# Query and key projections of the gated-memory mixer computed token-major, turned back through DRAM, with the modulation sums shared out differently

## The reference, cut to what matters

```python
proj = x @ w_in                                    # x [256, 2048]
qk, v, o, gates, z = split(proj)                   # qk has 2048 columns: 1024 for q, 1024 for k
qk = silu(causal_depthwise_conv(qk, conv_w, conv_b))   # 4 taps along the tokens, one filter a column
q, k = split(qk)                                   # 8 heads of 128 each
cell = mlstm_chunkwise(q, k, v, gates...)          # needs q and k with their features on the rows
...
mod = silu(c) @ w_ada + b_ada                      # one row of 6 * 2048 numbers for the second block
```

## Time and profile before

| | us |
|---|---|
| median of 3 runs | 2192.4 (2192.33 to 2195.02) |
| the profiled execution | 2195.33 |
| its span | 2193.4 |

### The profile page before, as it was taken

The page is one execution under the profiler, slowest core; times in us unless marked ns, Lnnn a source line. Parts: engine busy times, 40 slices in busy tenths (PEclk is TensorE's granted clock), DMA queues, the critical chain, the costliest instruction groups (busy, mean ns, idle before and its releaser), DMA issues.

```text
span 2193.4 us, 32090 instructions
## 1 busy us (share of the span) xinstructions
PE 2170.4 (99%) x10814; PEld 1840.6 (84%) x10814; DVE 1514.1 (69%) x2046; ACT 1019.5 (46%) x1251; POOL 297.4 (14%) x555
## 2 busy tenths in 40 slices
PE   9999999999999999999999999999999999999998
PEld 8898888988778887899888888888888888888886
DVE  6766668877777877688776768776666666554544
ACT  5445544554444546434555544454444444444433
POOL 2101110112220010701110211111111111000000
PEclk9999999999999999999999999999999999999999
DMA  8877577688996584968766887767878887765564
GB/s 291 240 193 245 174 260 245 198 227 287 299 297 190 176 303 143 263 204 263 229 187 193 285 277 239 237 222 237 268 253 278 268 260 241 224 233 185 190 198 139
DMA packets 204124, 512.22 MB, mean 234 GB/s; under 512 B 32704, under 2 KB 60000, under 8 KB 203744
## 3 DMA queue, kind: packets, MB, share of 16 engines
q1 hardware_dynamic: 166256, 394.10, 56.3%
q0 software_dynamic: 37456, 115.92, 16.6%
q10 hardware_dynamic: 288, 0.52, 0.1%
HBM read 502.58 MB, written 7.91 MB: 233 GB/s over the span
## 4 chain that ended last, share of the span: by engine, by line
PE 89%; DMA 4%; DVE 4%; ACT 1%; issue 1%; POOLq 0%; DVEq 0%; SPq 0%; ACTq 0%
PE ps L2361 72%; PE ps L2405 10%; DMA ada_raw<-in_w_ada_dram 3%; DVE lo L1307 1%; DMA raw<-in_ml_w_in_dram 1%; DVE acc_s L1319 1%; PE ps L2458 1%; PE ps L2831 1%; PE ps L2820 1%; PE ps L2719 0%; ACT hi L736 0%; DVE acc_g L1319 0%; PE ps L2553 0%; PE ps L2501 0%; PE ps L2554 0%
## 5 line engine op out<-in xcount | busy, mean ns | idle before, releaser
L1307 DVE TENSOR_TENSOR lo<-raw,hi 128x1024 fp32r<-128x1024 f32 x731 | 890.4, 1223 | 565.8 <-ACT hi L736 563.4
L736 ACT CAST hi<-raw 128x1024 fp32r<-128x1024 f32 x731 | 765.6, 1051 | 1004.0 <-PE ps L2361 769.5
L2361 PE MATMUL ps<-hi,XH 128*128 128x512 f32 x1944 | 607.7, 392 | 6.7 <-DVE lo L1307 4.4
L2361 PE MATMUL ps<-lo,XH 128*128 128x512 f32 x1944 | 602.0, 389 | 0.0
L2361 PE MATMUL ps<-hi,XL 128*128 128x512 f32 x1944 | 601.4, 389 | 0.0
L2361 PEld LDWEIGHTS ps<-hi,XH 128*128 128x128 f32 x1944 | 361.1, 188 | 83.0 <-issue 6.4
L2361 PEld LDWEIGHTS ps<-lo,XH 128*128 128x128 f32 x1944 | 364.9, 188 | 76.7
L2361 PEld LDWEIGHTS ps<-hi,XL 128*128 128x128 f32 x1944 | 364.9, 188 | 76.7
L625 POOL DMA_DIRECT2D ada_raw<-in_w_ada_dram x304 | 163.4, 539 | 1131.8 <-DVE acc_s L1319 848.5
L1319 DVE SCALAR_TENSOR_TENSOR acc_s<-ada_raw,c_act,acc_s 128x512 f32<-128x512 f32 x256 | 191.1, 747 | 21.8 <-DMA ada_raw<-in_w_ada_dram 20.4
L2405 PE MATMUL ps<-XH,hi 128*128 (+1 forms) x504 | 142.7, 283 | 0.0
(11 more groups left out here) (394 smaller groups left out, 1910.8 us busy)
## 6 DMA issues: line engine op xcount, KB each, us to landing
ada_raw<-in_w_ada_dram POOLq DMA_DIRECT2D x384, 256.0 KB, 4.7
raw<-in_w_in_dram SPq DMA_DIRECT2D x136, 512.0 KB, 4.5
raw<-in_ml_w_in_dram SPq DMA_DIRECT2D x128, 512.0 KB, 4.6
raw<-in_w_gate_dram SPq DMA_DIRECT2D x176, 256.0 KB, 3.0
raw<-in_w_up_dram SPq DMA_DIRECT2D x176, 256.0 KB, 3.4
raw<-in_w_down_dram SPq DMA_DIRECT2D x88, 512.0 KB, 4.3
raw<-in_mla_w_in_dram SPq DMA_DIRECT2D x47, 512.0 KB, 4.7
raw<-in_mla_w_out_dram SPq DMA_DIRECT2D x32, 512.0 KB, 4.6
```

Of the source, the lines that this page charges most:

```text
L736: nc.scalar.copy(hi[:, j, :], raw[:, j, :]).then_inc(hi_ready, 1)
L1307: nc.vector.tensor_tensor(lo[:, j, :], raw[:, j, :], hi[:, j, :].bitcast(F32), ALU.subtract) \
L2361: ins = mm(ps[:, o:o + HALF], x, w[:, b % RING, c0:c0 + HALF], start=first, stop=(k == n_rows - 1 and x is xl), skip_group_check=True)
```

## The change

- `mlq` and `mlk` are computed token-major. For the first block of `mlq` a new `token_first` takes the place of `feature_first`.
- When one of them is complete, VectorE turns its 128x2048 result in squares out of PSUM into `conv_turned`; this frees the PSUM half. POOL regroups it through DRAM into `conv_regrouped`, and ScalarE copies it into `conv_in` before block 15 of the next projection.
- The convolution of `mlq` now runs from SBUF beside `mv0`, and that of `mlk` beside `mv1`, one projection later than before.
- The sums are dealt anew: `mlk` 20 (was 4), `mv0` 10 (16), `mv1` 14 (20), `mo_0` 18 (20), `mo_1` 18 (20).
- On POOL the regroup of `mlq` stands before the clearing of `small_parts`, the loads of the gate weights, the start of `acc_g` and the issue of pieces from 80 on.

```diff
-REGROUPED = () + tuple(f"ffn{_p}" for _p in range(FFN_PASSES))
+REGROUPED = ("mlq", "mlk",) + tuple(f"ffn{_p}" for _p in range(FFN_PASSES))
...
-"... mlq@0:taps8 x1Tb:split4 mlk@1:taps8 mv0:act ..."
+"... mlq@0:dve x1Tb:split4 mlk@1:dve mv0:act ..."
...
-ADA_BESIDE = {... "mlq": 0, "mlk": 4, "mv0": 16, "mv1": 20, "mo_0": 20, "mo_1": 20, ...}
+ADA_BESIDE = {... "mlq": 0, "mlk": 20, "mv0": 10, "mv1": 14, "mo_0": 18, "mo_1": 18, ...}
...
+        conv_turned = at("conv_turned", 185, [P, ML_H * SEQ])
+        conv_regrouped = at("conv_regrouped", 160, [P, ML_H * SEQ])
+        conv_in = (at("conv_in0", 168, [P, ML_H, SEQ]), at("conv_in1", 193, [P, ML_H, SEQ]))
+        conv_rows = nc.dram_tensor("conv_rows", [2, P, ML_H * SEQ], F32, kind="Internal").ap()
...
 # POOL
             ada_units(0, 5)
+            ada_to(ADA_FIRST["mlk"] + RING)
             pool.wait_ge(ev("x1_rows"), 4)
+            regroup("mlq", conv_regrouped[:, :], conv_turned[:, :], conv_rows[0])
             nc.gpsimd.memset(small_parts[:, :, :, :].bitcast(F32), 0.0).then_inc(ev("small_zero"), 1)
             for q in range(4):
                 load("small2", gate_raw[:, 4 * q:4 * q + 4, :], ...)
                 if q == 1:
                     init_acc(acc_g[:, :], 2 * D, D, 12)
                 if q:
-                    ada_to(80 + 2 * q)
-            ada_to(96)
+                    ada_to(ADA_FIRST["mlk"] + 5 + 2 * q + RING)
+            ada_to(ADA_FIRST["mv0"] + RING)
+            regroup("mlk", conv_regrouped[:, :], conv_turned[:, :], conv_rows[1],
+                    lambda: ada_to(ADA_FIRST["mv0"] + 4 + RING))
+            ada_to(ADA_FIRST["mv1"] + RING)
             pool.wait_ge(*complete("gates"))
...
 # ScalarE
+            def conv_copy(q):
+                act.wait_ge(*rows_of(("mlq", "mlk")[q]))
+                nc.scalar.copy(by_quarter(conv_in[q], 0, ML_H), quarters(conv_regrouped[:, :])) \
+                  .then_inc(ev("conv_copied"), 1)
             first4(B_CONV + 16)
-            turn("mlq")
-            rest_blocks(B_CONV + 16, 4, 16, conv_before(0))
+            rest_blocks(B_CONV + 16, 4, 15)
+            conv_copy(0)
+            rest_blocks(B_CONV + 16, 15, 16)
...
 # VectorE
+            def turn_result(name, dst):
+                g = turn(name)
+                turn_squares(dst, ps[:, g:g + 4 * HALF].rearrange("p (t n) -> p t n", t=TOK), 8, freed_sem["dve"])
             first4(B_CONV + 16)
-            turn("mlq")
-            rest_blocks(B_CONV + 16, 4, 16, 16, "mlk", before=conv_before(0))
+            turn_result("mlq", conv_turned[:, :])
+            rest_blocks(B_CONV + 16, 4, 16, 16, "mlk")
             first4(B_VOZ)
-            turn("mlk")
+            dve.wait_ge(*rows_of("mlq"))
+            turn_result("mlk", conv_turned[:, :])
-            rest_blocks(B_VOZ, 4, 10, 16, "mv0", before=conv_before(1))
+            rest_blocks(B_VOZ, 4, 10, 16, "mv0", before=conv_before(0))
...
-            rest(B_VOZ + 16, 16, "mv1")
+            rest_blocks(B_VOZ + 16, 4, 16, 16, "mv1", before=conv_before(1))
+            dve.wait_ge(taps_done, 16)
...
 # TensorE
-            feature_major("mlq", B_CONV, 16, XH, XL, x1_tiles, blocks=(0, 5), hi_first=True)
+            token_first("mlq", B_CONV, x1_tiles)
+            token_major("mlq", B_CONV, 16, XH, XL, x1_tiles, blocks=(1, 5))
...
-            feature_major("mlq", B_CONV, 16, XH, XL, x1_tiles, blocks=(5, 16))
-            feature_major("mlk", B_CONV + 16, 16, XH, XL)
+            token_major("mlq", B_CONV, 16, XH, XL, x1_tiles, blocks=(5, 16))
+            token_major("mlk", B_CONV + 16, 16, XH, XL)
```

More of the change, by code:

```diff
@@ L84 @@
     "kn1@0:act v0@1:act v1@0:act z0@1:act mo0@1:dve mo1@0:dve "
-    "ada1a@1:act x1Ta@1:split5 mlq@0:taps8 x1Tb:split4 mlk@1:taps8 mv0:act gates:dve mv1@1:act mo_0:act mo_1:act mz0:act mz1@0:act "
+    "ada1a@1:act x1Ta@1:split5 mlq@0:dve x1Tb:split4 mlk@1:dve mv0:act gates:dve mv1@1:act mo_0:act mo_1:act mz0:act mz1@0:act "
     "yTa:split8 lo0:dve yTb:split8 lo1@1:dve "
@@ L129 @@
         TURN_COUNT[_name] = len(TURN_COUNT) + 1
-ADA_BESIDE = {"z1": 16, "kv": 12, "z0": 16, "mo0": 16, "mo1": 14, "mlq": 0, "mlk": 4, "mv0": 16, "mv1": 20, "mo_0": 20,
-              "mo_1": 20, "mz0": 6, "mz1": 6, "lo0": 8, "lo1": 10,
+ADA_BESIDE = {"z1": 16, "kv": 12, "z0": 16, "mo0": 16, "mo1": 14, "mlq": 0, "mlk": 20, "mv0": 10, "mv1": 14, "mo_0": 18,
+              "mo_1": 18, "mz0": 6, "mz1": 6, "lo0": 8, "lo1": 10,
               "qa": 8, "kb": 12, "vb": 16, "ga0": 12, "ga1": 12, "gb0": 12, "gb1": 16, "oa0": 6, "ob0": 6, "oa1": 6,
@@ L367, in two_block_kernel @@
         THREES = ("mo1", "down1")
+        FROM_PSUM = ("mlq", "mlk")
         def squares_of(name):
-            return ev("squares_turned"), REGROUPED.index(name) + 1
+            if name in FROM_PSUM:
+                return freed_sem["dve"], FREED[name][1]
+            return ev("squares_turned"), [n for n in REGROUPED if n not in FROM_PSUM].index(name) + 1
         def rows_of(name):
@@ L648, in ada_to, with regroup @@
                     ada_sent[0] = m + 1
-            def regroup(name, dst, src, scratch):
+            def regroup(name, dst, src, scratch, meanwhile=lambda: None):
                 n = src.shape[1] // 4
@@ L700, in _ @@
                          .rearrange("(p n) -> p n", p=32), cst("zeros", 64 * half + 32 * end, 64 * half + 32 * end + 32))
-            ada_units(6, 10)
-            ada_units(10, 12)
+            ada_to(16 * 7)
+            ada_units(7, 12)
             pool.wait_ge(*complete("ada1"))
@@ L1815, in _ @@
                                     gate_columns(0).bitcast(F32), ALU.subtract).then_inc(ev("small_lo"), 1)
-            rest_blocks(B_VOZ, 10, 16, 16, "mv0", before=conv_before(1))
+            rest_blocks(B_VOZ, 10, 16, 16, "mv0", before=conv_before(0))
             g = turn("gates")
@@ L1844, in _ @@
             nc.vector.tensor_tensor(select[:, :, :], one, two, ALU.add).then_inc(ev("heads_ready"), 1)
+            dve.wait_ge(ev("conv_copied"), 2)
+            for tok in range(TOK):
+                mark(nc.vector.memset(mv[:, tok, :, ML_V:ML_V + 1], 1.0))
             rest(B_VOZ + 32, 16, "mo_0")
@@ L2407, in feature_block, with token_first, feature_major @@
                 ins.then_inc(block_done, 1)
[L2409 removed]
+            def token_first(name, n0, need):
+                g = start(name)
                 pe.wait_ge(hi_ready, n0 + 1)
                 pe.wait_ge(*need(0))
[L2413 removed]
+                for w, x in ((hi, XH), (hi, XL), (lo, XH)):
                     if w is lo:
                         pe.wait_ge(lo_ready, n0 + 1)
[L2416 to L2419, removed]
+                    for tok in range(TOK):
+                        for c in range(2):
+                            o = g + (2 * tok + c) * HALF
+                            ins = mm(ps[:, o:o + HALF], x[:, 0, tok * P:(tok + 1) * P], w[:, 0, c * HALF:(c + 1) * HALF],
+                                     start=w is hi and x is XH, stop=False, skip_group_check=True)
                 ins.then_inc(block_done, 1)
[L2422 removed]
+            def feature_major(name, n0, nb, H, L, need=None, blocks=None):
                 b0, b1 = blocks or (0, RING)
                 g = start(name) if b0 == 0 else grp(name)
[L2427 to L2429 removed]
+                for b in range(b0, b1):
                     pe.wait_ge(lo_ready, n0 + b + 1)
```

30 lines of the change are left out of this document (16 added, 14 removed).

## The result

The changed kernel takes 2203.8 us (median of 6 runs, 2203.1 to 2205.1); the kernel before, beside it on the same chip, 2192.5 (2191.8 to 2196.3, 6 runs). The ratio is 1.0047, with a 95% interval of 1.0038 to 1.0057: slower by about 11 us, where I had forecast 2193.2 with a range to 2200. The prediction was wrong in its time. The profiled execution took 2205.1 with a span of 2203.4, 10.0 more than the span before.

The account below looks back on a forecast made before the run. TensorE, busy 99% of the span, was taken to bound the kernel. Gains of 5.1, 0.4 and 4.0 us against losses of 8.3 and 2.0 made it 0.8 slower: 2193.2 against 2192.4, range 2187.5 to 2200.

Parts of the forecast that it names:

- TensorE's own work: In `mlq` and `mlk`, 32 token-major blocks take 2.72 us each instead of 2.88: 5.1 us gained.
- `mv0`: Beside `mv0`, VectorE has 10 sums instead of 16, so its gap goes: 0.4 us gained.
- `mo_0`, `mo_1`: In `mo_0` and `mo_1`, 18 sums instead of 20 let late gaps go: 4.0 us gained (2.5 to 4.8).
- stall in `mlk`: TensorE stops before `mlk`'s block 9 as piece 80 comes late; with later waits and clock 8.3 us lost (4 to 14).
- `mv1`: In `mv1`, taps from SBUF bring VectorE to 3.18 us a block against 2.72: 2.0 us lost (1.3 to 3.5).
- The longest gap: Before `mlk`'s block 9, TensorE waits for `lo` queued behind the sums of late pieces 80 and 81: 5.8 us.
- The gaps after it: Later in `mlk`, pieces come one after another and `lo` 11 and 13 are late: 1.3 us more.
- the second rival: In `mlk`, a saturated DMA (361 GB/s asked, above 330) makes the stall 12 to 14 us: 2197 to 2199, chance 0.17.
- The clock: After the stall in `mlk`, TensorE runs one block at the lower clock, partly hidden: 1.2 us lost.
- The copies on ScalarE: Before block 15 of `mlk` and `mv0`, ScalarE's copies of regrouped rows find their read-backs landed: cost nothing.
- the third rival: In `mlq` and `mlk`, token-major steps shrink less, gaining 1.0 us instead of 5.1: 2197.3, chance 0.06.
- The rival of a hidden wait: The wait in `mlk` does not reach TensorE: 2184.9 without stall, 2188.9 with 4 us; chance 0.17, hidden or nearly so.

Follow-up runs that it names:

- e2: The kernel before with `mlq` and `mlk` computed token-major and nothing else (convolution reads its input in the wrong order): 2188.1 us, ratio 0.9975.
- e3: The changed kernel with POOL's clearing, two gate loads and `acc_g` start ahead of `mlq`'s earlier write, and pieces up to 83 issued while it lands: 2195.7 us.
- e4: The changed kernel with `mlq`'s read-backs taken from weight rows, not waiting for the write, which is still made (wrong data): 2203.1 us, ratio 1.0041.
- e8: The kernel before with only its sums dealt anew: `mv1` 16, `mo_0` and `mo_1` 18, `mz0` and `mz1` 8, `lo0` 10, `lo1` 12: 2187.7 us.
- e6: The changed kernel with sums redealt: `mlk` 8, `mv0` 12, `mv1` 8, `mz0` and `mz1` 12, `lo0` 10, `lo1` 12; gate loads before pieces 80 to 83: 2184.9 us.
- e7: e3 with the deal of sums of e6, the read-backs standing behind piece 79 instead of 83: 2184.7 us, ratio 0.9959.
- e10: The changed kernel in its own order, the convolution's two regroupings moving an eighth of their bytes, into a buffer cleared before: 2202.4 us, ratio 1.0039.
- e9: e6 with the deal of sums of the kernel before (`mlk` 4, `mv0` 16, `mv1` 20, `mo_0` and `mo_1` 20): 2199.1 us, ratio 1.0026.
- e5: e3 with the convolution's two regroupings moving an eighth of their bytes, into a buffer cleared before: 2190.2 us, ratio 0.9981.
- e1: The changed kernel with POOL's clearing, two gate loads, `acc_g` start and pieces up to 83 between `mlq`'s write and the wait for it: 2196.7 us.

## Why the prediction was wrong

| term | predicted | measured in the changed kernel |
|---|---|---|
| TensorE's own work | -5.1 | -2.6 in `mlq`, and as much taken for `mlk`; all of e2 is -5.3 |
| `mv0` | -0.4 | +0.1 (one gap of 0.32 for one of 0.22) |
| `mo_0`, `mo_1` | -4.0 | -4.8 |
| stall in `mlk` | +8.3 | +17.7 |
| `mv1` | +2.0 | +3.0 (2.03 in six gaps, and 0.16 each) |
| sum | +0.8 | +10.8; the span grew by 10.0, and the 0.8 between is not traced |

The step that failed is the size of the stall in `mlk`, 8.3 us forecast and 17.7 measured. Its mechanism was right up to the block: piece 79 behind sum 75, the write next, TensorE's stop before block 9, the clock at half behind it. Its three parts were all too short:
- **The longest gap**, 9.4 with its 0.16 instead of 5.8. Up to the write POOL was nearly on my times (+10.3 from the start of `mlk`, forecast +9.8). The write then took 9.6 from issue to POOL's next instruction, not 5.0. I took the row nearest in kind, from a stretch where little else moved, and not the one nearest in size; beside `mlk` even 7.9 was too little. e3's write, made 5 us earlier, landed in 5.1. Piece 80 then landed in 3.1 us instead of 4.7, which hid 1.6 of the error. The write's length alone does not make the stall, as e4 shows: without the wait for it the gap is still 7.36, because pieces land later.
- **The gaps after it**, 4.2 us plus 0.3 for the 0.16 of each, instead of 1.3, before blocks 12 and 13. I let pieces come 4.7 after their issue; in `mlk` their median was 5.6 and the longest 12.0, and the weight blocks' median 6.3 instead of 4.2 before. This is the second rival, added to my step, not in its place: I had weighed them as alternatives, and the range held one or the other.
- **The clock**, 3.7 instead of 1.2. It is what is left of the 17.7 after 14.0 us of gaps; the slow steps account for 3.5 of it, five pairs behind each of two gaps in 4.12 and 3.92 us instead of 2.27. The windows show a granted clock of 0.72, 0.50 and 0.75, the middle one the lower level of 1.2 GHz, and pairs of matmuls follow each other by 0.85 instead of 0.45. The third gap brought a second spell (0.66 between 460 and 465). I had one block at the low level, hidden in half behind `lo`.

My bound for this term, 14, was built from a write of 7.9 and pieces of 7. The write passed it with 9.6; the pieces passed it singly, with 12.0 at most, while their median stayed below.

The rest stood. In `mv1` a block took 3.23 against my 3.18, because three taps from SBUF cost 1.43, as from PSUM; I had taken 1.28 of 1.16 to 1.43. The copies on ScalarE, which I had put at nothing, cost nothing in `mlk`. In `mv0` a cast waited 6.7 us for its weight block (until 504.67), and 0.3 reached TensorE; that the second regrouping delayed the block is likely, not shown. The late gaps went with a tenth fewer sums, and e8 shows that by itself. The smaller step of the third rival is refuted by the trace (six pairs in 2.72 us), and e2's interval leaves out its gain of 1.0.

The rival "slower, by a saturated DMA" gave 2197 to 2199. Taken alone it comes nearest to what e3 shows: 2195.7, a stall with the engines at 1.0. The rival of a hidden wait gave 2184.9, and that is where nearly the same code arrives (e6, e7) once the deal leaves VectorE something in the ring. That the figures agree to the digit is luck: the rival was 7.5 below a kernel before of 2192.4, while e6 is 8.8 below one of 2193.7, and e6 has also lost the gaps of `mv1` that the rival kept.

What stays open is what the bytes weigh in the late order: 1.4 us by the medians, some 2 more if e10's clearing is taken off (an estimate), and 5.5 by the profiled executions, of which the changed kernel's is its longest and e10's its shortest. Open is also how much of the pieces' late landing is the read-backs' doing. In e10 they moved an eighth and pieces still took up to 11.0 us to land, perhaps behind weight blocks that SP issues in a row once TensorE goes on; that cause is argued, not shown.

## What to carry to other kernels

Before a DMA and a wait are put into a queue that also feeds a ring, count how long the ring lasts: buffers in it, divided by what its consumer takes per block. 18 us without an issue cost a gap of 9 us at 20 sums a result, and 17 us cost none at 8. And when an in-order engine serves both a side job and the main one, move the side job away from the result beside which new transfers are placed, not towards it. The best kernels here, e6 and e7, are 8.8 and 8.9 us (0.4%) faster than the one before: the changed one with part of its side job dealt to where the DMA engines' share was 0.7. Moving all of it away is no rule either: where the new transfers are queued behind a step of the side job, as here behind sum 75, too few steps make them late (e9).

## What the runs showed of the hardware

- Its size does not say how long a DMA takes to land. The same 1 MB write took 9.3, 8.1, 6.9 and 5.1 us to land in the changed kernel, e4, e6 and e3, and one of 128 KB 5.2 in e10 against 2.7 in e5. The Trainium skill (page "DMA: Bandwidth & Descriptors", section "Anatomy of one DMA — SWDGE (gpsimd) path") has a fit that gives an estimated 4.4 and 2.3 for these sizes. The 5.1 of e3 and the 2.7 of e5 come near it; the changed kernel's 9.3 and e10's 5.2 are twice as long.
- The share of the DMA engines does not order these times: it was 0.74 during e10's write and 0.83 during e5's shorter one, 0.99 during both 9.3 and 6.9 us (changed kernel, e6). The order on POOL's queue does: in the early order (e3, e7) 1 MB took 5.1 and 5.9 us, in the late one, where a piece had been issued 0.9 us ahead, 6.8 to 9.3 (changed kernel, e1, e4, e6, e9). That the piece is the reason is not shown.
- A DMA share near 1 does not mean one bandwidth. The four read-backs, each into 32 partitions, are under way in e3 between 435 and 440, and the engines move 248 GB/s there at a share of 1.03, where weights and pieces reach 330 at the same share.
- A stall costs more than itself: of the 17.7 us in `mlk`, 3.7 are TensorE at the lower clock after it had already gone on.
- VectorE's transposes of 128x512 from PSUM follow each other by 0.61 us (2.50 for four, the last lasting 0.68); forecast 0.66.
